# The Strassen feed-forward of a two-layer encoder step: four combined tiles, product order and one low half rearranged

## The reference

```python
def conv_ffn(h, w_in, conv_w, conv_b, w_out, pad):
    T = h.shape[1]
    u = h @ w_in
    up = jnp.concatenate([pad.astype(u.dtype), u], axis=1)
    c = conv_b + sum(up[:, j:j + T] * conv_w[j] for j in range(CONV_W))
    g, val = jnp.split(c, 2, axis=-1)
    y = (jax.nn.silu(g) * val) @ w_out
    return y, up[:, up.shape[1] - (CONV_W - 1):]
```

## Time and profile before

| what | us |
|---|---|
| median of 3 runs (3251.31 to 3253.42) | 3251.47 |
| the profiled execution | 3248.83 |
| its span in the trace | 3247.0 |
| PE busy | 2993.8 (92%) |
| DVE busy | 2178.7 (67%) |
| POOL busy | 1650.1 (51%) |
| ACT busy | 1238.0 (38%) |

### The profile page before, as it was taken

How to read it: one execution, slowest core, us unless ns; L and a number is a source line. 1 busy time by engine, 2 the same in 40 slices (tenths; PEclk the granted TensorE clock), 3 DMA queues, 4 the chain that set the end, 5 groups by cost and what they waited for, 6 DMA issues and landing times.

```text
span 3247.0 us, 47471 instructions
## 1 busy us (share of the span) xinstructions
PE 2993.8 (92%) x18469; PEld 2876.1 (89%) x18469; DVE 2178.7 (67%) x3257; ACT 1238.0 (38%) x2590; POOL 1650.1 (51%) x1023
## 2 busy tenths in 40 slices
PE   7999999896999999999987999999699999999998
PEld 6888888796999998999977888889699999999997
DVE  6666666347888887335776777762888888833465
ACT  5555555223333332113340666651333333311243
POOL 2222221325899994222334778753499999622231
PEclk8999999898999999999988999999899999999999
DMA  5222222312222224211104121221122222422111
GB/s 113 69 68 72 68 66 91 104 40 73 70 73 68 73 67 152 101 60 55 39 24 121 34 59 51 94 82 46 64 69 73 70 70 72 156 79 78 59 39 62
DMA packets 284366, 237.37 MB, mean 73 GB/s; under 512 B 29988, under 2 KB 266228, under 8 KB 284148
## 3 DMA queue, kind: packets, MB, share of 16 engines
q1 hardware_dynamic: 269336, 220.43, 22.5%
q10 hardware_dynamic: 14812, 13.97, 1.4%
HBM read 170.20 MB, written 64.16 MB: 72 GB/s over the span
## 4 chain that ended last, share of the span: by engine, by line
PE 61%; DVE 13%; POOL 11%; issue 6%; ACT 5%; DMA 3%; SPq 0%; ACTq 0%; POOLq 0%; DVEq 0%
PE ps L1150 17%; PE ps L1152 16%; PE ps L1151 16%; POOL t L934 6%; PE ps L1333 2%; ACT t L1916 2%; PE ps L1468 2%; PE ps L1286 2%; PE ps L1269 2%; DVE t L2351 1%; POOL t L962 1%; POOL t L953 1%; PE ps L1353 1%; DVE t L2366 1%; DMA t<-in_w_ffn_in 1%
## 5 line engine op out<-in xcount | busy, mean ns | idle before, releaser
L1150 PE MATMUL ps<-t,t 128*128 128x384 f32 (+1 forms) x4760 | 1601.1, 336 | 136.9 <-POOL t L889 53.8
L1152 PE MATMUL ps<-t,t 128*128 128x384 f32 (+1 forms) x4760 | 1566.6, 329 | 0.0
L1151 PE MATMUL ps<-t,t 128*128 128x384 f32 (+1 forms) x4760 | 1565.3, 329 | 0.0
L1150 PEld LDWEIGHTS ps<-t,t 128*128 128x128 f32 x4760 | 903.8, 190 | 177.5 <-POOL t L889 55.5
L1151 PEld LDWEIGHTS ps<-t,t 128*128 128x128 f32 x4760 | 904.8, 190 | 1.0 <-issue 0.2
L1152 PEld LDWEIGHTS ps<-t,t 128*128 128x128 f32 x4760 | 903.2, 190 | 0.0
L934 POOL TENSOR_TENSOR t<-t,t 128x512 fp32r<-128x512 f32 x320 | 542.0, 1719 | 20.0 <-ACT t L2024 10.7
L889 POOL TENSOR_TENSOR t<-t,t 128x1024 fp32r<-128x1024 f32 x101 | 249.0, 2465 | 455.5 <-ACT t L1803 452.2
L2024 ACT ACTIVATE t<-t 128x512 fp32r<-128x512 f32 x320 | 198.0, 631 | 526.8 <-POOL t L942 218.8
L2698 DVE TENSOR_TENSOR t<-t,ps 128x384 f32<-128x384 f32 (+1 forms) x240 | 126.3, 531 | 279.6 <-PE ps L1152 279.6
L883 POOL TENSOR_TENSOR t<-t,t 128x1024 fp32r<-128x1024 f32 x51 | 106.0, 2079 | 266.5 <-PE ps L1152 266.0
(11 more groups left out here) (191 smaller groups left out, 4119.4 us busy)
## 6 DMA issues: line engine op xcount, KB each, us to landing
t<-in_w_ffn_in SPq DMA_DIRECT2D x160, 256.0 KB, 2.9
ff_dram<-t SPq DMA_DIRECT2D x44, 544.0 KB
t<-ff_dram SPq DMA_DIRECT2D x44, 544.0 KB, 6.8
t<-in_w_ffn_out SPq DMA_DIRECT2D x44, 512.0 KB, 3.4
t<-in_w_qkv_a SPq DMA_DIRECT2D x24, 512.0 KB, 3.9
t<-in_w_ple_gate SPq DMA_DIRECT2D x16, 512.0 KB, 3.8
out<-t SPq DMA_DIRECT2D x32, 192.0 KB, 2.1
t<-in_w_o_a SPq DMA_DIRECT2D x8, 512.0 KB, 4.0
```

What stands on the lines that cost most here:

```text
L1150: pe.matmul(out, a_hi, b_hi, start=start, stop=False, skip_group_check=True)
L1151: pe.matmul(out, a_hi, b_lo, start=False, stop=False, skip_group_check=True)
L1152: return pe.matmul(out, a_lo, b_hi, start=False, stop=stop, skip_group_check=True)
```

## The change

The three taps of the filter stay on VectorE. Around them:

- T4 has four buffers (two in other words of memory), is made by VectorE (`combined_fourth`) and not by GpSimd, and each k has its own store semaphore.
- GpSimd splits chunk c0+2 ahead of all combinations, and c0+3 behind the first of them. The copies and high halves on ScalarE, and the filters on VectorE, stand in a new order.
- In a pair the products run A11, A11, S3, A21, A22, A22, S2, S1, A12, A12, S4. A22's slot becomes free after `blk_done` + 4 (before: 6), A12's after 7.
- The low half of A12 is made by VectorE (`last_low`), between the filter of the gate half and the gate.
- The first four gated tiles are loaded into `ff_first`, in the words of the first activations' low halves, ahead of weight chunk `down_chunk(0, 1)`.

```diff
             def ffn_weights(l):
 
                 c0 = at[f"F{l}"][0]
                 split(c0 + 1, ffn=l)
+                split(c0 + 2, ffn=l)
                 combine(l, 0)
-                combine(l, 1)
-                split(c0 + 2, ffn=l)
-                combine(l, 2)
-                combine(l, 3)
                 split(c0 + 3, ffn=l)
+                for k in range(1, 4):
+                    combine(l, k)
...
                     else:
                         sp.wait_ge(blk_done, BLK_DONE + done + 1)
                         down_chunk(0, 0)
                         store_tile(n + 1)
-                        sp.wait_ge(blk_done, BLK_DONE + done + 5)
-                        down_chunk(0, 1)
+                        sp.wait_ge(blk_done, BLK_DONE + done + 4)
                         sp.wait_ge(ff_stored, FF_STORED + 16 * (f0 + 8))
                         load_tiles(0)
+                        sp.wait_ge(blk_done, BLK_DONE + done + 6)
+                        down_chunk(0, 1)
                         load_tiles(1)
...
                         load_block("A21", n + 1)
                         store_tile(n + 1)
-                        sp.wait_ge(blk_done, BLK_DONE + done + 6)
+                        sp.wait_ge(blk_done, BLK_DONE + done + 4)
                         load_block("A22", n + 1)
...
+                def combined_fourth(k):
+
+                    dve.wait_ge(comb_made, COMB_MADE + 12 * l + 3 * k + 3)
+                    if k == 2:
+                        stored, before = comb_stored[0]
+                        dve.wait_ge(stored, before + 32 * (l + 1))
+                    dve.tensor_tensor(t4_raw[k], parts[k % 2][2], t_raw[1][:, k, :], ALU.subtract).then_inc(comb_hn, 1)
...
+                def last_low(n):
+
+                    m = PAIRS * l + n
+                    hi, lo, raw = slots[l]["A12"]
+                    dve.wait_ge(s_made, S_MADE + 4 * m + 4)
+                    dve.wait_ge(blk_high, BLK_HIGH + 8 * m + 7)
+                    dve.tensor_tensor(lo, raw, hi.bitcast(F32), ALU.subtract).then_inc(sums_made, 1)
...
                     if more:
                         loaded_high("A22", n + 1)
+                        made_high("S2", n + 1, 2)
+                        made_high("S1", n + 1, 3)
                     else:
                         for k in range(4):
                             tile_high(0, k)
                     act.wait_ge(part_done, PART_DONE + 2 * m + 2)
                     act.wait_ge(conv_step, 3 * unit)
                     act.activation(ubuf[0][:, 2:386], ps[:, 0, 0:384], ACT.Copy).then_inc(u_kept, 1)
-                    if more:
-                        made_high("S2", n + 1, 2)
```

The opening of the feed-forward on ScalarE is new as a whole:

```diff
                 kept(0, 0)
+                kept(0, 1)
+                kept(1, 0)
+                kept(1, 1)
+                act.wait_ge(chunk_done, c0 + 1)
+                weights_high(c0 + 2, 0)
+                kept(0, 2)
+                weights_high(c0 + 3, 0)
                 combined_high(0)
-                kept(0, 1)
+                kept(1, 2)
+                kept(2, 0)
                 combined_high(1)
...
+                kept(2, 1)
+                kept(2, 2)
                 combined_high(2)
...
+                kept(3, 0)
                 combined_high(3)
```

More of the change, by code:

```diff
@@ L691, in ffn @@
                 sp.wait_ge(gemm_done, g0 + 8)
-                sp.wait_ge(comb_stored, COMB_STORED + 128 * (l + 1))
+                for stored, before in comb_stored:
+                    sp.wait_ge(stored, before + 32 * (l + 1))
                 sp.dma_start(h_hi[:, 0:4, 384:768].bitcast(F32), t4h_dram).then_inc(t4_loaded, 16)
@@ L956, in pair_weights @@
                 block_rest("A21", 2)
+                block_rest("A22", 4)
                 pool.wait_ge(blk_loaded["A12"], BLK_LOADED + 16 * (m + 1))
                 if n:
-                    pool.wait_ge(blk_done, BLK_DONE + 8 * (m - 1) + 7)
+                    pool.wait_ge(blk_done, BLK_DONE + 8 * (m - 1) + 8)
                 else:
@@ L1570, in pair @@
                     product(5, "A12", h_second[:, :, 768:T], l_second[:, :, 768:T], False).then_inc(blk_done, 1)
+                    pe.wait_ge(blk_split, BLK_SPLIT + 7 * m + 7)
+                    pe.wait_ge(sums_made, SUMS_MADE + 6 * m + 5)
+                    product(3, "S4", h_second[:, :, 384:768], l_second[:, :, 384:768], False).then_inc(blk_done, 1)
                 def down(j):
@@ L2014, in combined_high @@
                 def combined_high(k):
-                    made = 16 * l + 4 * k
+                    made = 12 * l + 3 * k
                     for i, t in enumerate((0, 2, 1)):
@@ L2079, in pair @@
                     more = n < PAIRS - 1
[L2080 to L2085 removed]
+                    if n:
+                        first_copied(n)
+                        loaded_high("A12", n)
+                        made_high("S4", n, 4)
+                        sigmoid(n + 1, unit - 1)
                     if more:
                         loaded_high("A11", n + 1)
+                        loaded_high("A21", n + 1)
+                        made_high("S3", n + 1, 1)
                     else:
@@ L2090, in pair @@
                         weights_high(c0 + 4, 0)
-                    if n:
-                        sigmoid(n + 1, unit - 1)
-                    if more:
-                        loaded_high("A21", n + 1)
-                        made_high("S3", n + 1, 1)
-                    act.wait_ge(blk_done, BLK_DONE + 8 * m + 6)
+                    act.wait_ge(blk_done, BLK_DONE + 8 * m + 4)
                     act.wait_ge(conv_step, 3 * (unit - 1) if n else 3 * unit)
@@ L2132, in ffn @@
                 made_high("S3", 0, 1)
-                kept(3, 1)
+                sigmoid(0, u0 + 1)
                 loaded_high("A22", 0)
+                kept(3, 2)
                 made_high("S2", 0, 2)
+                first_copied(0)
                 made_high("S1", 0, 3)
-                sigmoid(1, u0 + 2)
-                kept(3, 2)
+                loaded_high("A12", 0)
+                made_high("S4", 0, 4)
+                sigmoid(1, u0 + 3)
                 for n in range(PAIRS):
                     pair(n)
-                act.wait_ge(blk_done, BLK_DONE + 8 * (PAIRS * (l + 1) - 1) + 7)
+                act.wait_ge(blk_done, BLK_DONE + 8 * (PAIRS * (l + 1) - 1) + 8)
                 weights_high(c0 + 5, 0)
@@ L2715, in ffn @@
                 filtered(u0 + 3, 1, 1, 12)
+                last_low(0)
                 gate_tile(1, u0 + 3)
```

159 lines of the change are left out of this document (76 added, 83 removed).

## The result

The changed kernel takes 3304.4 us in the median of 4 runs (3301.8 to 3307.3) against 3251.8: a ratio of 1.016, interval 1.014 to 1.018. That is 51 us above the forecast of 3253, and 28 above the end of its range. The profiled execution took 3301.8, its span is 3300.0, 53.0 over that of before.

The account below looks back on a forecast made before the run. VectorE and its turns with GpSimd were taken to bound the changed kernel, at 23.5 us a pair. 3248.8 + 7 (pairs) + 0 (openings) - 4 (hand-over) = 3252, as median 3254, said 3253; range 3212 to 3276.

Parts of the forecast that it names:

- The load behind the store: In each pair A22's load waits behind the gated tile's store; the store adds 0.5 us, making a pair 23.5 us.
- The closed chain over two pairs: Successive pairs, late then back in phase: a late S1 sum delays TensorE's next first product; two pairs cost 46.9 us.
- VectorE and the turns are the bound: In the pairs VectorE, alternating with GpSimd on SBUF operations, has no idle left; they set the pace, not TensorE's 21.6 us.
- Rival 2: A22's load late in each pair (store adds over 0.75 us): 23.9 us a pair, 3270 us in all; chance 0.22.
- The ring rule: One ring's descriptors go in order, so A22's load waits for the store's whole data: 1.0 us, a 23.9 us pair.
- The alternation: TensorE's first products of successive pairs stand alternately 22.5 and 24.4 us apart.
- The openings at 0: In the feed-forward openings most of 53.8 us of TensorE waits go, yet 0 gained, within 8 us each direction for both.
- new waits forecast for TensorE: In the openings TensorE would newly wait before c0+3's second segment, pair 0 and its A22; no size given.
- The hand-over: Before the down-projection, the first tiles load earlier into their own buffer: 2.1 us less a layer, 4 in all.
- The first of the nineteen gaps: From first to last gate, nineteen pairs counted, the first called short; all priced at 23.5 us, 446.5 together.
- VectorE idle by 2 us in a pair: Sign of a wrong forecast, in the pairs: VectorE idle that long would mean its turns with GpSimd are not the bound.
- rival 3: In the pairs VectorE's and GpSimd's turns collide less: 22.2 us a pair, 3205 us in all; chance 0.16.

Follow-up runs that it names:

- the run with bank 0 ahead: Against the changed kernel, ScalarE's copy of bank 0 put back ahead of the next pair's S1 high half, bank 5's copy still behind: 3302.0 us (1.015).
- both orders mended: Against the changed kernel, S1's high half behind the copies of banks 0 and 5, and A22's load ahead of the store: 3222.9 us (0.991).
- the last run: The kernel before, its pairs kept, with the changed feed-forward opening and hand-over (tile loads only after `blk_done` + 6): 3252.1 us (1.000).

## Why the prediction was wrong, by its steps

**The step that failed** is the one in "The load behind the store" that puts S1's high half in front of the bank copies and goes on from there. A pair costs 24.8, not 23.5: 2 x 19 x 1.3 = 49 us more than forecast, nearly the whole error. Two terms of the step were wrong.

*TensorE behind its gap.* The closed chain over two pairs is in the prediction, in three legs: 16.2 from the restart to VectorE's sum of bank 3 ("15.7 of TensorE work and some 0.5 of restart and drain"), 21.2 from there to the gate, 9.4 to the next restart, with rounding its 46.9. Measured over sixteen turns of both layers: 17.3 to 18.8, 21.3 to 22.7, and 9.3 to 9.5; in the mean 17.9, 22.3 and 9.3. The largest miss is the first leg. The eight products of it took 15.75 us from 1063.04, where TensorE had not stopped, 17.4 from 1039.70 behind 3.16 us of waiting, and 18.2 from 990.52 behind 4.21: the granted clock was 0.50 in the 5 us after the latter (rows in the last section). I had paid for the slow clock in the openings and put it at nothing in the pairs. The 1.1 us of the second leg, VectorE's turns, were not taken apart.

*The copy of bank 5.* I followed what the new order does to the next pair's first product and stopped there. The same order holds the copy of bank 5, and with it VectorE's gate-half filter, which I let start at once ("VectorE is through 22.1"). With the numbers of the prediction itself: S1 sum ready at 22.1 + 1.16 = 23.3, high half 23.9, bank 0 24.4, bank 5 some 0.5 more, 24.9. VectorE would have been ready at 22.1 + 0.5 for its sum, 22.6. It waits 2.3 us; measured 2.12. In the changed kernel this wait is hidden by the later one for TensorE. But with TensorE in time it comes in each pair and holds it at 24.65 (the run with bank 0 ahead), so the forecast would have been missed even with the right clock.

**"VectorE and the turns are the bound"** was wrong for this kernel: VectorE waits 28.6 us in 300 and GpSimd idles 70. It was right once the chain is broken: 293 of 300 us busy, and 22.55 a pair. These 293 hold VectorE's waits for its turns. With only S1's high half moved it is busy 265 in pairs of the same length, and waits 15.4 us for the S4 sum and 12.7 for the sigmoid: the chain shown there happens to be as long as VectorE's work with its turns.

**The load behind the store.** Rival 2 named this place as the slower side, with 0.8 a pair and by the order of turns. The load takes 3.48 us from issue to the S2 sum at 1034.31 and 3.24 a pair earlier (store 1003.90, load 1004.74, sum 1007.98), against 2.9 in the earlier trace rows, and 3.61 in the run with bank 0 ahead (1005.73 to 1009.34): the store adds 0.35 to 0.7, and I had taken 0.5. The ring rule that the prediction names from the Trainium skill (DMA: Bandwidth & Descriptors, "Queues, rings and completion order") would by its 1.0 end have made the pair 23.9; the load in the trace pays about half of that. So the size was right and the consequence was not. The price lies in SP's order, not in the store's data: SP waits for the gate before it comes to the load, and with the load first it goes out 6.4 us before the gate's end (1007.09 against 1013.47 with both orders mended), and the edit alone is worth 79 us.

**The alternation** was forecast as 22.5 and 24.4; measured are 23.8 and 25.6 in the mean of layer 0 from 865 us on. Its kind was right, both its steps were too short, by 1.2 to 1.4.

**The openings at 0** held: +1.9 and -1.4, and the last run shows it alone. Of the new waits forecast for TensorE all three are there, in layer 0 (timeline of TensorE):

```profile
762.32 0.69 PE L1152 MATMUL ps<-t,t 128*128 128x384 f32 x1 [6.35 <-ACT t L2077]
...
783.14 0.69 PE L1152 MATMUL ps<-t,t 128*128 128x384 f32 x1 [10.70 <-POOL t L938]
...
798.33 0.66 PE L1152 MATMUL ps<-t,t 128*128 128x384 f32 x1 [5.21 <-DMA t<-t_low_dram]
```

They are c0+3's second segment, pair 0 and its A22: 22.3 us together, in place of 26.2, of which the earlier trace rows show 13.84. The reason that I gave was only half right: a gate 1.5 us earlier is given back in the next gap, so it isn't VectorE's gate alone that everything hangs on.

**The hand-over** gained 1.5 and 1.2 us, for 2.1 forecast.

**The first of the nineteen gaps** is called short in the prediction. In the kernel before it is the longest: 804.3 to 830.9, 26.6 us, and 24.4 in layer 1, against 23.13. In the changed kernel it is 25.0 and 24.9, hardly longer than the others, so that nineteen equal gaps were a fair sum for it; that was luck.

**The range** ended at 3276. Its far end took a load that is late in each pair, 0.8 us dearer; no case in it had TensorE slow behind its gap, or an engine idle by 2 us because of another engine's order, although the prediction itself lists "VectorE idle by 2 us in a pair" as a sign of being wrong. I read that sign as the side of rival 3, with turns that collide less.

## What to carry to other kernels

When an instruction is moved ahead of others on an in-order engine, list everyone that waits for each instruction it is now in front of, not only the engine on which the change is meant to help; here TensorE's copy was counted and VectorE's, right behind it, was not. Price TensorE's work behind a gap of 3 to 4 us with the slow clock in it, here 1.7 to 2.5 us. Then follow the latest of them round to see if it comes back to its own start: a closed chain (gate, store, load, sum, sum, high half, copy, filter, gate) costs its whole length in each turn, whatever room the engines have. Two such chains can be nearly equal, and to mend one shows nothing then. Break them at the cheapest link that they share, here one 0.63 us instruction or one transfer issued ahead of another, and only then look at which engine is full.

## What was not expected of the hardware

- A `tensor_scalar` over two columns is not free of GpSimd's turns. In one pair of the changed kernel the two tails together take 0.23 us while GpSimd is idle, and 1.32 while it makes low halves (timeline of VectorE):

```profile
1032.71 0.23 DVE L2660 TENSOR_SCALAR t<-t 128x2 f32<-128x2 f32 x2
...
1041.03 1.32 DVE L2660 TENSOR_SCALAR t<-t 128x2 f32<-128x2 f32 x2
```

- Behind the gap of 4.21 us before 990.52 in the changed kernel TensorE's granted clock was 0.50 for 5 us, the level of 1.2 of 2.4 GHz, and half as many matmuls ran in them as in the next five (busy time by stretch, PEclk third last):

```profile
990.50:995.50 5.00, 4.98 (x16) 5.00 (x17) 4.67 (x5) 1.03 (x4) 4.92 (x5) 0.50 0.00 0
995.50:1000.50 5.00, 5.00 (x32) 5.00 (x32) 4.96 (x3) 1.66 (x3) 5.00 (x3) 0.97 0.20 56
```

  From 900 to 1200 us it was 0.95 in the mean in this kernel, with gaps of 3.1 to 4.2 us in every second pair, 0.98 with gaps of 1.1 to 2.4 in each pair (the run with bank 0 ahead), and 1.00 in the kernels with no gap over 1.2 us. TensorE's busy time in a pair went with it: 22.9 us (277.1 in 12.1 pairs), against 22.0 before (285.0 in 13.0) and 21.7 with the tap on ScalarE. So a gap costs TensorE more than its own length.
- The tap as an activation with scale and bias takes 1.30 us on ScalarE for 1090 columns, against 0.84 to 1.90 on VectorE, and doesn't take part in the turns.
